# Two halves of a gate weight in one stationary operand, added afterwards by a folding matrix

## The chip, the cores and the metric

The kernel runs on one core of one Trainium2 chip. The metric is the device time of one execution in microseconds (us), the median of three. A core has five engines that run side by side and meet through semaphores: TensorE (PE; its weight loads are listed apart as PEld), VectorE (DVE), ScalarE (ACT), GpSimd (POOL) and SyncE (SP), which here only issues DMAs. Each engine works through its own queue strictly in the order of the program.

## The reference

A decoder trunk of two layers over 256 positions of width 1024. Layer 0 is native sparse attention (NSA): 16 heads in 4 groups, three branches (compressed blocks, selected blocks, sliding window), and three learned gates per head that weight the branches:

```
proj = h @ w_in                      # h = rms_norm(x, norm_w)
q, kc, vc, ks, vs, kw, vw, gl, z = split_cols(proj, ...)
gates = sigmoid(gl)                  # gl: 256 positions x 48 (16 heads x 3)
o = gates0 * o_cmp + gates1 * o_sel + gates2 * o_win
x = x + (o * silu(z)) @ w_out
```

Layer 1 is an HGRN2 gated recurrence with its own input and output projections; a final RMS norm follows. The change touches only `gl` and the sigmoid, 48 columns of the first projection.

## The kernel before, in words

Every large product is made in a split form. A float32 weight tile is copied by ScalarE into a rounded `w_hi` (type fp32r, line 826), VectorE writes the remainder `w_lo = raw - w_hi` (line 1073), and the activations are split in the same way into `h_hi` and `h_lo`. The product is the sum of three passes, hi by hi, hi by lo and lo by hi. The weights come as 19 units of 1024 x 512 through two landing buffers; SyncE may load a unit only when the unit two before it has been split.

One list, `SCHEDULE`, sets the order of all work. It is written out by hand as two strings (`ORDER`, `H_ORDER`), one letter a step, and every engine walks through the same list, doing at each step its own share. Each step fills one of eight PSUM banks; `filled` and `drained` semaphores, one pair a bank, tie TensorE to the engine that empties it. Places for the splits of coming units are given as step numbers, so on ScalarE and VectorE they stand in line with the draining of banks.

The norm's per-position factor `rstd` is not put into `h`: it is a column on positions (`stat[:, 0, 2]`), and a row of it, `rs_row`, serves the outputs that are held transposed.

The steps around the change, in order of the list:

- `wg` (1024 x 48) is loaded (line 509), split by ScalarE (1007) and VectorE (1220).
- `gl` (line 675): for each of 8 slices of the depth, three matmuls with a stationary operand of 48 columns and 256 positions moving: 24 in all, into bank 7, partitions 0 to 47. VectorE multiplies the bank by `rs_row` (1226) and ScalarE writes the sigmoid to `gT` (911).
- `cmpT 0` (659): the compression MLP's hidden layer, whose two halves of 64 partitions are added and transposed in one matmul against `fold`, a 128 x 64 matrix with ones where the partition modulo 64 equals the column. ScalarE takes it with Silu (907).
- `stage 2`: a rotated key tile is transposed (648) and copied out by ScalarE (894).
- `glT` (681): two transposes bring `gT` back to positions x 48; ScalarE copies them to `gate` (914), VectorE masks one branch (1253). The first use of `gate` otherwise is in the attention (1101).
- Then the query units `U_Q0` and `U_Q1`; each of their four tiles passes VectorE (rope, 1194 to 1202), GpSimd (sum, 1427), ScalarE (hi part, 884), GpSimd (lo part, 1435) and is then transposed by TensorE (`stage 4` to `stage 7`). `cmpT 1`, with its Silu, stands between `stage 4` and `stage 5`.
- Line 946 is the exponential of the attention's scores, the first of them at step `s 0`.

Which function set ScalarE has loaded is not written in the kernel: the compiler puts an ACT_TABLE_LOAD ahead of an activation whose function is not in the set that is loaded. Copy never needs one here.

Of the kernel before, what the change touches and what calls it, by code (L numbers as in the profile page):

```python
# [21 lines left out]
P = 128  # L22
D = 1024
S = 256
KT = D // P
TT = S // P
UW = 512
H, G, R, HD = 16, 4, 4, 64
# [9 lines left out]
F32 = mybir.dt.float32  # L38
FR = mybir.dt.float32r
BF16 = mybir.dt.bfloat16  # L40
U8 = mybir.dt.uint8
ALU = mybir.AluOpType
ACT = mybir.ActivationFunctionType
# [3 lines left out]
NSA_Q, NSA_KC, NSA_KS, NSA_KW, NSA_GL, NSA_Z = 0, 1024, 1536, 2048, 2560, 2608  # L47
# [177 lines left out]
def program(nc, t_in, out):  # L225
    with ExitStack() as ctx:
        def sb(name, shape, dt=F32, scope=ctx):
            return scope.enter_context(nc.sbuf_tensor(name, shape, dt))
# [6 lines left out]
        h_hi = sb("h_hi", [P, KT, S], FR)  # L235
        h_lo = sb("h_lo", [P, KT, S], FR)
        g_row = sb("g_row", [P, D])
        g_cols = sb("g_cols", [P, KT])
        ident = sb("ident", [P, P])
        ident_r = sb("ident_r", [P, P], FR)  # L240
        fold = sb("fold", [P, HD])
# [11 lines left out]
        stat = sb("stat", [P, 3, 5, TT])  # L253
# [5 lines left out]
        gate = sb("gate", [P, TT, 48])  # L259
        ostat = sb("ostat", [P, TT, 3, 8])  # L260

        nsa = ExitStack()
# [12 lines left out]
        rs_row, ones = scratch[:, 0:S], scratch[:, S:S + P]  # L275
# [3 lines left out]
        pre = ExitStack()  # L279
# [4 lines left out]
        kcr = sb("kcr", [P, 3, HD], F32, pre)  # L284
        tri = kcr[:, 0:2].rearrange("p a d -> p (a d)")
        kcs = sb("kcs", [P, P], F32, pre)
        wg = sb("wg", [P, KT, 48], F32, pre)
        wg_hi = sb("wg_hi", [P, KT, 48], FR, pre)
        wg_lo = sb("wg_lo", [P, KT, 48], FR, pre)
        gT = sb("gT", [48, S], F32, pre)  # L290
        pre.close()
        att = ExitStack()
        prob_t = sb("prob_t", [P, 4, 512], F32, att)
# [28 lines left out]
        def sem(name):  # L322
            return ctx.enter_context(nc.semaphore(name))
# [13 lines left out]
        wg_in = sem("wg_in")  # L337
# [11 lines left out]
        fold_set = sem("fold_set")  # L349
# [5 lines left out]
        rstd = sem("rstd")  # L355
# [3 lines left out]
        diag_set = sem("diag_set")  # L359
        h0_hi = sem("h0_hi")  # L360
        kc_scaled = sem("kc_scaled")
        gl_scaled = sem("gl_scaled")
        z_scaled = sem("z_scaled")
        r_ab = sem("r_ab")
        r_sum = sem("r_sum")
# [2 lines left out]
        flat_zero = sem("flat_zero")  # L368
        kc_v = sem("kc_v")
        zeros = sem("zeros")  # L370
        wg_hi_d = sem("wg_hi_d")
        wg_lo_d = sem("wg_lo_d")
        gate_v = sem("gate_v")
# [27 lines left out]
        def wait_full(eng, key):  # L401

            b, k = USES[key]
            eng.wait_ge(filled[b], k + 1)

        def wait_taken(eng, key):

            b, k = USES[key]
            eng.wait_ge(drained[b], k + 1)

        def taken(key):
            return drained[USES[key][0]]
# [87 lines left out]
        @block.sync  # L500
        def _(sp):
            for u, (kind, col) in enumerate(UNITS):
                if u == 1:
                    sp.dma_start(rope[:], t_in["c_rope"]).then_inc(rope_in, 16)
                if u == NRAW:
                    for dst, src in CONST_LOADS:
                        sp.dma_start(dst, src).then_inc(const_in, 16)
                if u == NRAW + 1:
                    sp.dma_start(wg[:], t_in["nsa"][:, NSA_GL:NSA_Z].rearrange("(k p) n -> p k n", p=P)).then_inc(wg_in, 16)
                    load_w1(sp, "k")  # L510
                if u >= NRAW:

                    sp.wait_ge(lo_done, split_count(u - NRAW, KT - 1))
                dst = raw[:, u % NRAW]
                w = t_in[kind][:, col:col + UW]
                if kind == "nsa_out":

                    w = w.rearrange("(gp g2 r d) n -> g2 d gp r n", gp=2, g2=2, r=R)
                    for g2 in range(2):
                        for gp in range(2):  # L520
                            sp.dma_start(dst[g2 * HD:(g2 + 1) * HD, gp * R:(gp + 1) * R], w[g2][:, gp]).then_inc(raw_in[u % NRAW], 16)
                    continue
                w = w.rearrange("(k p) n -> p k n", p=P)
                if u == 0:

                    for kk in range(KT):
                        for t, part in {0: ((0, 0),), 1: ((1, 0),), 4: ((0, 1), (1, 1))}.get(kk, ()):
                            half = slice(part * UW, (part + 1) * UW)
                            sp.dma_start(x[:, t, half], t_in["x"][t * P:(t + 1) * P, half]).then_inc(x_in[t][part], 16)
                        sp.dma_start(dst[:, kk], w[:, kk]).then_inc(first_in[kk], 16)  # L530
                    continue
                for half in range(2):
                    landed = second_in[half] if u == 1 else raw_in[u % NRAW]
                    sp.dma_start(dst[:, 4 * half:4 * half + 4], w[:, 4 * half:4 * half + 4]).then_inc(landed, 16)
            for t in range(TT):
                sp.wait_ge(done_row, t + 1)
                sp.dma_start(out[t * P:(t + 1) * P, 0:UW], y_hg[:, t, 0:UW]).then_inc(out_done, 16)
            sp.wait_ge(out_done, 32 * TT)
# [7 lines left out]
        def _(pe):  # L546
            def mm(o, lhsT, rhs, start, stop):
                return nc.tensor.matmul(o, lhsT, rhs, start=start, stop=stop, skip_group_check=True)  # L548
# [16 lines left out]
            for n, (step, banks) in enumerate(SCHEDULE):  # L565
                kind = step[0]
                key = bank_key(step)
# [6 lines left out]
                b, k = USES[key]  # L574
                ps = bank[b]
# [5 lines left out]
                if kind == "hT":  # L581
                    _, L, t, q = step
# [7 lines left out]
                    for j in range(per_bank):  # L590
                        c = (per_bank * q + j) * P
                        m = nc.tensor.transpose(ps[:, j * P:(j + 1) * P], src[:, c:c + P], ident[:])  # L592
                elif kind == "gc":
                    pe.wait_ge(ident_in, 16)
                    pe.wait_ge(g_cols_in, 16)
                    m = nc.tensor.transpose(ps[:, 0:KT], g_rows[0:KT], ident[0:KT, 0:KT])
                elif kind == "rs":
                    pe.wait_ge(ones_set, 1)
                    pe.wait_ge(diag_set, TT)
                    for t in range(TT):  # L600
                        m = mm(ps[:, t * P:(t + 1) * P], ones, diag[:, t], t == 0, t == 1)
                elif kind == "pa" and step[1] == 0:

                    _, u, t, sl = step
# [6 lines left out]
                    for j, kk in enumerate(two):  # L611
# [3 lines left out]
                        m = mm(ps[:], h_lo[:, kk, t * P:(t + 1) * P], w_hi[:, u, kk], False, kk == KT - 1)  # L615
                elif kind == "pa":

                    _, u, t, sl = step
                    if sl == 0:
                        act_ready(0 if u <= U_O1 else 1, t, u)  # L620
                    for kk in (2 * sl, 2 * sl + 1):
# [4 lines left out]
                        m = mm(ps[:], h_lo[:, kk, t * P:(t + 1) * P], w_hi[:, u % 2, kk], False, kk == KT - 1)  # L626
# [48 lines left out]
                elif kind == "gl":  # L675
                    pe.wait_ge(wg_lo_d, 1)
                    for kk in range(KT):
                        mm(ps[0:48, 0:S], wg_hi[:, kk], h_hi[:, kk], kk == 0, False)
                        mm(ps[0:48, 0:S], wg_hi[:, kk], h_lo[:, kk], False, False)
                        m = mm(ps[0:48, 0:S], wg_lo[:, kk], h_hi[:, kk], False, kk == KT - 1)  # L680
                elif kind == "glT":
                    wait_taken(pe, ("gl",))
                    for t in range(TT):
                        m = nc.tensor.transpose(ps[:, t * 48:(t + 1) * 48], gT[:, t * P:(t + 1) * P], ident[0:48, 0:48])
                elif kind == "sc":
                    i = step[1]

# [127 lines left out]
        def _(act):  # L815
# [34 lines left out]
            for n, (step, _) in enumerate(SCHEDULE):  # L850
                kind, key = step[0], bank_key(step)
                if LAST.get(key) == n:
# [54 lines left out]
                        nc.scalar.activation(hidT[:, step[1]].rearrange("p c (g n) -> p (c g) n", g=G)[:, :, 0:CS],  # L907
                                             ps[:, 0:2 * HD].rearrange("p (c n) -> p c n", n=CS), ACT.Silu).then_inc(taken(key), 1)
                    elif kind == "gl":
                        act.wait_ge(gl_scaled, 1)  # L910
                        nc.scalar.activation(gT[:], ps[0:48, 0:S], ACT.Sigmoid).then_inc(taken(key), 1)
                    elif kind == "glT":
                        wait_full(act, key)
                        nc.scalar.activation(gate[:], ps[:, 0:TT * 48].rearrange("p (t c) -> p t c", t=TT), ACT.Copy).then_inc(taken(key), 1)
                    elif kind == "kcT":
                        wait_full(act, key)
                        nc.scalar.activation(kc_t[:], ps[:, 0:P], ACT.Copy).then_inc(taken(key), 1)
# [86 lines left out]
                            nc.scalar.activation(ostat[:, c, 1], ostat[:, c, 0], ACT.Sqrt, scale=1.0 / P, bias=eps_t[:]).then_inc(o_root, 1)  # L1004
                    if key == ("pb", U_KC, 1):
                        act.wait_ge(wg_in, 16)
                        nc.scalar.activation(wg_hi[:], wg[:], ACT.Copy).then_inc(wg_hi_d, 1)
                        act.wait_ge(const_in, 16 * N_CONST)
                        nc.scalar.activation(tri_b[:], tri, ACT.Copy).then_inc(idents, 1)
                    if key == ("pb", V_F0, 0):  # L1010
# [43 lines left out]
        def _(dve):  # L1054
# [11 lines left out]
            V = nc.vector  # L1066
# [82 lines left out]
            for n, (step, _) in enumerate(SCHEDULE):  # L1149
                kind, key = step[0], bank_key(step)  # L1150
                if LAST.get(key) == n:
# [52 lines left out]
                    elif key[0:2] == ("pb", U_KC):  # L1204
# [12 lines left out]
                        m.then_inc(taken(key), 1)  # L1217
                        if kv == 1:
                            dve.wait_ge(wg_hi_d, 1)
                            V.tensor_tensor(wg_lo[:], wg[:], wg_hi[:].bitcast(F32), ALU.subtract).then_inc(wg_lo_d, 1)  # L1220
                            step_(V.tensor_tensor(lb[:, 0], lbl[:, 0], lbl[:, 1], ALU.max))
                            settled()
                            V.tensor_tensor(lb[:, 1:3], lbl[:], bc(lb[:, 0], 2, 1), ALU.subtract).then_inc(lb_v, 1)
                    elif kind == "gl":
                        wait_full(dve, key)
                        V.tensor_tensor(ps[0:48, 0:S], ps[0:48, 0:S], rs_row[0:48], ALU.mult).then_inc(gl_scaled, 1)
                    elif kind == "pb" and step[1] in (U_Z0, U_Z1):
                        wait_full(dve, key)
                        both = lambda ap: ap.rearrange("p (j s) -> p j s", j=2)
# [175 lines left out]
        def _(pool):  # L1405
            GP = nc.gpsimd
            row = lambda ap: ap.unsqueeze(0).broadcast_to([P, D])
            GP.memset(hidT[:], 0.0).then_inc(zeros, 1)
            GP.memset(vc_bd[:], 0.0).then_inc(zeros, 1)

# [110 lines left out]
```

## Time and profile before

| | us |
|---|---|
| three runs | 330.66, 330.60, 330.00; median 330.6 |
| the profiled execution, its own time | 330.72 |
| its span, first to last instruction | 328.9 |
| TensorE busy | 317.3 (96%) |
| VectorE, ScalarE, GpSimd busy | 228.9, 188.6, 57.8 |
| mean granted clock of TensorE | 0.997 of full speed |

Busy time says how full an engine is, not what sets the end. The chain of waits does that: it follows the last instruction back, at each step to what released it. In the rows below the first column is the start of an instruction from the span's start in us, the second its duration in us; `x24` means 24 instructions merged; a bracket at the end gives idle time of the engine before it and what ended that. Line numbers (L548) are those of the kernel before; L548 is the helper that issues every matmul.

### The profile page before, as it was taken

To read this page: it belongs to the slowest core of one execution; us is meant where nothing else is said; L and a number is where in the kernel's file an instruction comes from. 1 tells how busy PE (TensorE), PEld (TensorE's weight loads), DVE (VectorE), ACT (ScalarE), POOL (GpSimd) and SP (SyncE) were. 2 spreads that over 40 slices of the span, in tenths; PEclk is the share of its full clock that TensorE was granted. 3 is DMA by queue.
4 is the path that set the end of the run, shared out by engine and by line. 5 is a ranking of instruction groups with operands and counts; after the bars stand their busy time and mean duration, and the time that the engine had idled before them with its cause. 6 is when DMAs were issued, how large, how long until landed. Compare 5 with 4: busy or idle time off the path is not lost.

```text
span 328.9 us, 6172 instructions
## 1 busy us (share of the span) xinstructions
PE 317.3 (96%) x2380; PEld 268.4 (82%) x2380; DVE 228.9 (70%) x400; ACT 188.6 (57%) x400; POOL 57.8 (18%) x55
## 2 busy tenths in 40 slices
PE   7999999999999999999999999999999999998993
PEld 5889778867989877777678878999999788897882
DVE  2789953649569978879828726277449988489824
ACT  4694355356696666668536706838345036898223
POOL 1004022070423443346300010100000011101000
PEclk9999999999999999999999999999999999999998
DMA  7999999806390920033270773653662424001011
GB/s 229 394 335 209 265 358 195 264 31 223 105 186 0 212 47 2 0 112 146 68 253 0 257 258 127 248 201 91 227 249 91 168 96 165 2 1 66 0 64 64
DMA packets 28828, 49.41 MB, mean 150 GB/s; under 512 B 3256, under 2 KB 7744, under 8 KB 28800
## 3 DMA queue, kind: packets, MB, share of 16 engines
q1 hardware_dynamic: 25760, 44.30, 42.9%
q10 hardware_dynamic: 2528, 2.69, 4.2%
q0 software_dynamic: 512, 2.03, 1.9%
q8 instruction: 19, 0.31, 0.4%
q14 instruction: 9, 0.07, 0.1%
HBM read 47.97 MB, written 1.05 MB: 149 GB/s over the span
## 4 chain that ended last, share of the span: by engine, by line
PE 66%; DVE 16%; ACT 5%; issue 2%; POOL 2%; ACTq 0%; DVEq 0%; POOLq 0%
PE bank L548 61%; DVE w_lo L1073 6%; ACT w_hi L826 3%; PE bank L727 3%; DVE nmax L1268 2%; POOL rp L1427 1%; PE bank L648 1%; DVE prob_t L1280 1%; DVE qk L1357 1%; DVE ft L1324 1%; DVE qk L1343 1%; PE bank L592 1%; DVE zT L1215 1%; DVE zT L1216 0%; ACT prob L946 0%
## 5 line engine op out<-in xcount | busy, mean ns | idle before, releaser
L1073 DVE TENSOR_TENSOR w_lo<-raw,w_hi 128x1024 fp32r<-128x1024 f32 (+1 forms) x80 | 89.2, 1159 | 34.8 <-ACT w_hi L826 34.7
L548 PE MATMUL bank<-w_hi,h_hi 128*128 128x512 f32 x192 | 77.9, 412 | 2.4 <-DVE h_lo L1172 1.1
L548 PE MATMUL bank<-w_hi,h_lo 128*128 128x512 f32 x192 | 75.2, 392 | 0.0
L548 PE MATMUL bank<-w_lo,h_hi 128*128 128x512 f32 x192 | 75.2, 392 | 0.0
L826 ACT ACTIVATE w_hi<-raw 128x1024 fp32r<-128x1024 f32 (+1 forms) x80 | 72.9, 967 | 2.1 <-issue 1.9
L548 PE MATMUL bank<-h_hi,w_hi 128*128 128x256 f32 x224 | 64.9, 290 | 0.1
L548 PE MATMUL bank<-h_hi,w_lo 128*128 128x256 f32 x224 | 63.5, 283 | 0.0
L548 PE MATMUL bank<-h_lo,w_hi 128*128 128x256 f32 x224 | 63.5, 283 | 0.0
L548 PEld LDWEIGHTS bank<-w_hi,h_hi 128*128 128x128 f32 x192 | 35.9, 188 | 11.4 <-issue 4.0
L548 PEld LDWEIGHTS bank<-h_hi,w_hi 128*128 128x128 f32 x224 | 43.0, 192 | 0.5 <-DVE w_lo L1073 0.3
L548 PEld LDWEIGHTS bank<-h_lo,w_hi 128*128 128x128 f32 x224 | 43.0, 192 | 0.3
L548 PEld LDWEIGHTS bank<-h_hi,w_lo 128*128 128x128 f32 x224 | 43.0, 192 | 0.0
L548 PEld LDWEIGHTS bank<-w_hi,h_lo 128*128 128x128 f32 x192 | 36.1, 188 | 7.9
L548 PEld LDWEIGHTS bank<-w_lo,h_hi 128*128 128x128 f32 x192 | 36.2, 188 | 6.8 <-DVE w_lo L1160 0.3
L470 POOL TENSOR_TENSOR prob<-prob,scl 128x512 f32<-128x512 f32 x24 | 28.0, 1166 | 38.9 <-DVE scl L1104 19.8
L946 ACT ACTIVATE prob<-bank,nmax 128x128 f32<-128x128 f32 (+1 forms) x64 | 26.2, 421 | 14.3 <-DVE nmax L1268 14.3
L1427 POOL TENSOR_TENSOR rp<-rp 128x256 f32<-128x256 f32 (+1 forms) x8 | 10.0, 1252 | 64.4 <-DVE rp L1197 44.3
L548 PEld LDWEIGHTS bank<-qk 128*64 128x64 f32 (+1 forms) x496 | 18.0, 140 | 3.8 <-issue 3.5
L548 PE MATMUL bank<-qk 128*64 128x32 f32 (+2 forms) x496 | 19.1, 225 | 0.8 <-DVE qk L1357 0.7
L1456 POOL TENSOR_TENSOR z_hg<-z_hg,g_row 128x512 f32<-128x512 f32 x4 | 5.2, 1301 | 78.9 <-ACT z_hg L967 78.9
L1268 DVE TENSOR_REDUCE nmax<-bank 128x2 f32<-128x512 f32 (+1 forms) x24 | 16.4, 685 | 3.0 <-PE bank L548 2.9
L1357 DVE TENSOR_TENSOR qk<-qk,ft 128x1024 f32<-128x1024 f32 x12 | 15.2, 1284 | 4.1 <-PE bank L548 4.1
(194 smaller groups left out, 424.3 us busy)
## 6 DMA issues: line engine op xcount, KB each, us to landing
raw<-in_hg SPq DMA_DIRECT2D x16, 1024.0 KB, 7.4
raw<-in_nsa SPq DMA_DIRECT2D x12, 1024.0 KB, 9.0
raw<-in_nsa_out SPq DMA_DIRECT2D x8, 512.0 KB, 8.5
raw<-in_hg_out SPq DMA_DIRECT2D x4, 1024.0 KB, 6.2
raw<-in_nsa SPq DMA_DIRECT2D x8, 256.0 KB, 5.9
w<-in_w1k SPq DMA_DIRECT2D x2, 1024.0 KB, 16.3
w<-in_w1v ACTq DMA_DIRECT2D x2, 1024.0 KB, 15.8
x_res<-in_x SPq DMA_DIRECT2D x4, 256.0 KB, 5.2
```

Source lines behind the costliest of these rows:

```text
L470: nc.gpsimd.tensor_tensor(v(pb_), v(pb_), bc(scl[:, it, 0:nb], 512 // nb, 2), ALU.mult).then_inc(scaled, 1)
L548: return nc.tensor.matmul(o, lhsT, rhs, start=start, stop=stop, skip_group_check=True)
L592: m = nc.tensor.transpose(ps[:, j * P:(j + 1) * P], src[:, c:c + P], ident[:])
L648: m = nc.tensor.transpose(ps[:, c * P:(c + 1) * P].bitcast(FR), stg[:, j % 2, 4 * half + c], ident_r[:])
L727: m = nc.tensor.transpose(ps[:, c * P:(c + 1) * P], prob[:, prob_slot(it), c * P:(c + 1) * P], ident[:])
L826: m = nc.scalar.activation(dst, src, ACT.Copy)
L946: m = nc.scalar.activation(prob[:, prob_slot(it), c * w:(c + 1) * w], ps[:, c * w:(c + 1) * w], ACT.Exp, bias=nmax[:, it, c:c + 1], accum_ ...
L1073: m = V.tensor_tensor(lo, src, hi.bitcast(F32), ALU.subtract)
L1268: V.tensor_reduce(nmax[:, it, 0:nb], ps[:].rearrange("p (a b) -> p a b", a=nb), AX.X, ALU.max, negate=True).then_inc(rowmax, 1)
L1357: V.tensor_tensor(both, both, decay, ALU.mult).then_inc(qk_up, 1)
L1427: GP.tensor_tensor(rp[:, 2, 0:w], rp[:, 0, 0:w], rp[:, 1, 0:w], ALU.add).then_inc(r_sum, 1)
L1456: GP.tensor_tensor(zs, zs, g_row[:, (u - V_Z0) * UW:(u - V_Z0 + 1) * UW], ALU.mult).then_inc(z_g, 1)
```

## The change

The high and the low part of the gate weight are put side by side into one tile `wg_r`, 64 columns each (48 of weights, 16 of zeros that GpSimd writes at the start). One matmul with this 128-column operand gives both halves at once, the high part's product on partitions 0 to 47, the low part's on 64 to 111; it is made with `h_hi` and with `h_lo`. ScalarE copies the bank out unscaled. In `glT` a matmul against the first 48 columns of `fold` adds the halves and transposes. `rstd` is now a per-partition scale of the sigmoid, which therefore comes behind `glT`, once for each 128 positions.

```diff
-        wg = sb("wg", [P, KT, 48], F32, pre)
-        wg_hi = sb("wg_hi", [P, KT, 48], FR, pre)
-        wg_lo = sb("wg_lo", [P, KT, 48], FR, pre)
-        gT = sb("gT", [48, S], F32, pre)
+        wg = sb("wg", [P, KT, HD], F32, pre)
+        wg_r = sb("wg_r", [P, KT, 2, HD], FR, pre)
+        gT = sb("gT", [P, S], F32, pre)
...
                 elif kind == "gl":
                     pe.wait_ge(wg_lo_d, 1)
                     for kk in range(KT):
-                        mm(ps[0:48, 0:S], wg_hi[:, kk], h_hi[:, kk], kk == 0, False)
-                        mm(ps[0:48, 0:S], wg_hi[:, kk], h_lo[:, kk], False, False)
-                        m = mm(ps[0:48, 0:S], wg_lo[:, kk], h_hi[:, kk], False, kk == KT - 1)
+                        both = wg_r[:, kk].rearrange("p a c -> p (a c)")
+                        mm(ps[:, 0:S], both, h_hi[:, kk], kk == 0, False)
+                        m = mm(ps[:, 0:S], both, h_lo[:, kk], False, kk == KT - 1)
                 elif kind == "glT":
                     wait_taken(pe, ("gl",))
+                    pe.wait_ge(fold_set, 1)
                     for t in range(TT):
-                        m = nc.tensor.transpose(ps[:, t * 48:(t + 1) * 48], gT[:, t * P:(t + 1) * P], ident[0:48, 0:48])
+                        m = mm(ps[:, t * 48:(t + 1) * 48], gT[:, t * P:(t + 1) * P], fold[:, 0:48], t == 0, t == TT - 1)
...
                     elif kind == "gl":
-                        act.wait_ge(gl_scaled, 1)
-                        nc.scalar.activation(gT[:], ps[0:48, 0:S], ACT.Sigmoid).then_inc(taken(key), 1)
+                        wait_full(act, key)
+                        nc.scalar.activation(gT[:], ps[:, 0:S], ACT.Copy).then_inc(taken(key), 1)
                     elif kind == "glT":
                         wait_full(act, key)
-                        nc.scalar.activation(gate[:], ps[:, 0:TT * 48].rearrange("p (t c) -> p t c", t=TT), ACT.Copy).then_inc(taken(key), 1)
+                        act.wait_ge(rstd, TT)
+                        nc.scalar.activation(gate[:, 0], ps[:, 0:48], ACT.Sigmoid, scale=stat[:, 0, 2, 0:1])
+                        nc.scalar.activation(gate[:, 1], ps[:, 48:96], ACT.Sigmoid, scale=stat[:, 0, 2, 1:2]).then_inc(taken(key), 1)
...
                         act.wait_ge(wg_in, 16)
-                        nc.scalar.activation(wg_hi[:], wg[:], ACT.Copy).then_inc(wg_hi_d, 1)
+                        act.wait_ge(wg_pad, 1)
+                        nc.scalar.activation(wg_r[:, :, 0], wg[:], ACT.Copy).then_inc(wg_hi_d, 1)
...
-                            V.tensor_tensor(wg_lo[:], wg[:], wg_hi[:].bitcast(F32), ALU.subtract).then_inc(wg_lo_d, 1)
+                            V.tensor_tensor(wg_r[:, :, 1], wg[:], wg_r[:, :, 0].bitcast(F32), ALU.subtract).then_inc(wg_lo_d, 1)
...
-                    elif kind == "gl":
-                        wait_full(dve, key)
-                        V.tensor_tensor(ps[0:48, 0:S], ps[0:48, 0:S], rs_row[0:48], ALU.mult).then_inc(gl_scaled, 1)
...
+            GP.memset(wg[:, :, 48:HD], 0.0).then_inc(wg_pad, 1)
             GP.memset(hidT[:], 0.0).then_inc(zeros, 1)
```

The load of `wg` writes 48 of each 64 columns; otherwise it is as before.

## Rows read from the trace of the kernel before

**Rows 1.** Page, part 4: shares of the chain that ended last, by engine

```profile
PE 66%; DVE 16%; ACT 5%; issue 2%; POOL 2%; ACTq 0%; DVEq 0%; POOLq 0%
```

**Rows 2.** Chain of waits, 40 to 92 us: start, duration, engine and line

```profile
40.63 15.28 PE bank L548 x96
...
56.20 0.25 PE bank L684 x2
...
74.36 0.28 ACT hid L900
...
75.87 5.98 PE bank L548 x28
...
85.75 0.30 PE bank L648 x4
```

**Rows 3.** Timeline of TensorE around 22, 50 and 56 us (start, duration, ...)

```profile
21.57 0.28 PE L548 MATMUL bank<-h_lo,w_hi 128*128 128x256 f32 x1
...
22.27 0.28 PE L548 MATMUL bank<-h_lo,w_hi 128*128 128x256 f32 x1
...
48.38 0.12 PEld L548 LDWEIGHTS bank<-h_lo,wg_hi 128*48 128x48 f32 x1
...
50.95 0.12 PEld L548 LDWEIGHTS bank<-h_hi,wg_lo 128*48 128x48 f32 x1
...
51.18 0.55 PE L548 MATMUL bank<-fold,hid 128*128 128x64 f32 x4
...
51.54 0.48 PE L548 MATMUL bank<-w_hi,h_hi 128*128 128x512 f32 x1
...
56.13 0.32 PE L684 MATMUL bank<-ident,gT 48*128 48x48 f32 x2
...
56.38 0.54 PE L648 MATMUL bank<-ident_r,stg 128*128 128x128 f32 x4
```

**Rows 4.** Timeline of ScalarE, 51 to 62 us

```profile
51.84 0.38 ACT L911 ACTIVATE gT<-bank 48x256 f32<-48x256 f32 x1 [2.05 <-DVE bank L1226]
...
52.23 1.28 ACT L907 ACT_TABLE_LOAD   x1
...
53.53 0.28 ACT L907 ACTIVATE hidT<-bank 128x128 f32<-128x128 f32 x1
...
58.09 0.24 ACT L914 ACTIVATE gate<-bank 128x96 f32<-128x96 f32 x1
...
61.88 0.60 ACT L894 ACTIVATE k<-bank 128x512 fp32r<-128x512 f32 x1 [3.05 <-PE bank L648]
```

**Rows 5.** One source line, L962 (F: sigmoid, Q: silu, in turn)

```profile
L962 ACT ACT_TABLE_LOAD  x4: 1283/1283/1283, 207.2 to 242.3; - x4
```

**Rows 6.** Timeline of ScalarE, 77 to 84 us

```profile
77.25 0.60 ACT L894 ACTIVATE q<-bank 128x512 fp32r<-128x512 f32 x1
77.72 0.29 ACT L907 ACTIVATE hidT<-bank 128x128 f32<-128x128 f32 x1
77.88 1.17 ACT L826 ACTIVATE w_hi<-raw 128x512 fp32r<-128x512 f32 x2
...
83.27 0.63 ACT L884 ACTIVATE stg<-rp 128x512 fp32r<-128x512 f32 x1 [3.73 <-POOL rp L1427]
```

**Rows 7.** Timeline of VectorE, 63 to 80 us

```profile
63.39 0.75 DVE L1194 SCALAR_TENSOR_TENSOR rp<-bank,stat,rope 128x512 f32<-128x512 f32 x1 [3.04 <-PE bank L548]
...
79.08 1.29 DVE L1073 TENSOR_TENSOR w_lo<-raw,w_hi 128x512 fp32r<-128x512 f32 x2 [0.23 <-ACT w_hi L826]
80.29 0.75 DVE L1194 SCALAR_TENSOR_TENSOR rp<-bank,stat,rope 128x512 f32<-128x512 f32 x1
```

**Rows 8.** Timeline of GpSimd, 81 to 86 us

```profile
81.90 1.28 POOL L1427 TENSOR_TENSOR rp<-rp 128x512 f32<-128x512 f32 x1 [8.07 <-DVE rp L1202]
83.98 1.30 POOL L1435 TENSOR_TENSOR stg<-rp,stg 128x512 fp32r<-128x512 f32 x1 [0.80 <-ACT stg L884]
```

**Rows 9.** Timeline of TensorE's weight loads, 85 us

```profile
85.40 0.51 PEld L648 LDWEIGHTS bank<-ident_r,stg 128*128 128x128 f32 x4
```

More of the change, by code:

```diff
@@ L361, in program @@
         kc_scaled = sem("kc_scaled")
-        gl_scaled = sem("gl_scaled")
         z_scaled = sem("z_scaled")
@@ L370, in program @@
         zeros = sem("zeros")
+        wg_pad = sem("wg_pad")
         wg_hi_d = sem("wg_hi_d")
@@ L508, in _ @@
                 if u == NRAW + 1:
-                    sp.dma_start(wg[:], t_in["nsa"][:, NSA_GL:NSA_Z].rearrange("(k p) n -> p k n", p=P)).then_inc(wg_in, 16)
+                    sp.dma_start(wg[:, :, 0:48], t_in["nsa"][:, NSA_GL:NSA_Z].rearrange("(k p) n -> p k n", p=P)).then_inc(wg_in, 16)
                     load_w1(sp, "k")
```

## The prediction, made before the changed kernel was run

> **What bounds the kernel now.** I read the page's chain by engine first: TensorE holds 66% of it, VectorE 16%, ScalarE 5% [rows 1]. So a matmul saved is worth something only where TensorE's work is the piece that ends last, and a ScalarE instruction costs something only where it delays such a piece. Next the chain in order of time. From 40.63 us TensorE is on it without a break for 15.28 us, which takes in the gate's 24 matmuls, and the two gate transposes at 56.20 are on it as well. Then a stretch runs through VectorE, GpSimd and ScalarE and comes back through `hid` at 74.36; from 75.87 TensorE has it again, the transposes of `stage 6` at 85.75 among them [rows 2]. The reader is to see that everything the change touches lies within this half, and that the chain starts each link from TensorE: VectorE's rope at 63.39 waited 3.04 us for a TensorE bank [rows 7]. No DMA holds a share of the chain [rows 1].
>
> **What is removed on TensorE.** The 24 gate passes follow one another every 0.117 us: the second weight load starts at 48.38, the last at 50.95, 22 steps, 2.57 us [rows 3]. Would a full operand of 128 columns be slower? Passes of just that form (128 columns held, 256 moving) near 22 us stand at 21.57 and 22.27 with six steps between: 0.117 us as well [rows 3]. So the width costs nothing, the 16 passes take 1.87 us where 24 took 2.81, and 0.94 us goes. If the wider load cost something, the gain would be less; bound from below nothing, from above 0.94. I take 0.94, since the row is of the same form.
>
> **What is added in `glT`.** Two transposes become two float32 matmuls against `fold`. The same form with 64 moving columns stands at `cmpT 0`: it starts at 51.18 and the next work at 51.54, 0.36 us for two calls (four instructions). The old pair took from 56.13 to 56.38, 0.25 us [rows 3]. That is +0.11; with 48 columns a little less. I take +0.1 (bounds 0 and +0.2). TensorE is then 0.84 us early from 56.4 on.
>
> **Edits with cost nothing.** VectorE loses the product with `rs_row`, and ScalarE no longer waits for it; both stood idle there (ScalarE 2.05 us before `gT` [rows 4]), so nothing is gained. The two wider splits of `wg` add a third to one instruction each, long before `gl`, and the pad memset is GpSimd's first instruction, on an engine with nothing to do then. The new waits (`fold_set`, `wg_pad`, `rstd`) are for things done tens of microseconds earlier. The `wg` load moves the same bytes. If TensorE's later work should come to wait for a split, the wider split costs at most about 0.15 us.
>
> **The function sets of ScalarE.** Before, the order is sigmoid (`gl`), silu (`cmpT 0`), silu (`cmpT 1`), exp. Between sigmoid and silu there is a load of 1.28 us at 52.23, and between the two silus none: at 77.72 the second follows the copy at 77.25 directly [rows 4, 6]. After the change the order is silu (`cmpT 0`), sigmoid (`glT`), silu (`cmpT 1`), exp. Could one set hold both functions? Layer 1 changes from sigmoid to silu, back, and over again, and line 962 has four loads for it [rows 5]; so no set that the compiler picks holds both, in either direction. The number of loads thus goes up by one, and two stand in new places.
>
> The first, ahead of the sigmoid, meets idle time. `gate` was written at 58.09 and after the next copy ScalarE waited 3.05 us for TensorE, until 61.88 [rows 4]. A load (1.28) and one more activation (about 0.3) fit into 3.05; without that cover they would cost 1.6. Queued behind them are one key copy, whose reader comes much later, and VectorE's mask and its small key work, followed by a wait of 3.04 us [rows 7]. The copy of `gT` needs no load, so the silu behind it comes earlier than before. Nothing is lost here.
>
> The second, ahead of the silu of `cmpT 1`, does not. ScalarE is busy without a gap there. Before, the silu starts 0.47 us after the copy at 77.25, overlapping it. A load does not overlap: at 51.84 `gT` ran 0.38 us, the load began at 52.23, and the next activation at 53.53, 1.30 us later [rows 4]. So the silu will start 0.60 + 1.30 = 1.90 us after the copy starts, 1.43 us later than it did [rows 6]. Behind it in ScalarE's queue stands the split at 77.88, and what follows has no slack at all: VectorE waited 0.23 us for that split and starts the remainder at 79.08; its rope at 80.29 stands directly behind [rows 7]; GpSimd waited 8.07 us for the rope and starts at 81.90 [rows 8]; ScalarE waited 3.73 us for GpSimd and starts the hi part at 83.27 [rows 6]; GpSimd makes the lo part from 83.98 to 85.28 [rows 8]; and TensorE loads the operand of `stage 6` at 85.40 [rows 9], 0.12 us after. Other such releases take about 0.07, so TensorE had 0.05 us to spare.
>
> **The sum.** ScalarE comes to 77.25 earlier by 0.84 (the whole chain up to there starts from TensorE) and leaves the silu later by 1.43: net +0.59 at the split, and this +0.59 is handed along to 85.28. Less the 0.05 of slack, `stage 6` starts 0.54 us later than before, though TensorE is ready for it 0.84 us earlier: it will stand idle some 1.4 us between 82 and 86. `stage 6` is on the chain [rows 2], so +0.54 goes to the end: 330.72 + 0.54 = 331.26 on the profiled execution, which is 0.12 above the median of the runs; on the median, 331.1 us. The own range of this case is +0.2 to +0.9: the gain at TensorE may be 0.74 to 0.94, and the load's 1.28 may overlap its neighbours by some tenths.
>
> **A rule weighed.** What the rows show is a load of 1.28 us with the next activation 0.02 us behind its end [rows 4]. The Trainium skill, ScalarE: Activation LUTs, section "What ACT_TABLE_LOAD costs", gives the same 1283 ns but adds a drain of about 1380 ns, some 2.66 us for each switch, and its section on table sets says to batch calls by set, which this change undoes. By that price the sum would be an estimate of +1.9 us, 332.5. The trace has no such drain at this place, so I give it little.
>
> **The rivals.**
> - A. The second load does not reach TensorE: a set with both functions is found, or the split behind the silu has more room than I see. Then only TensorE's gain is left, 330.6 - 0.84 = 329.8. For it: TensorE's 0.84 is sure. Against it: four loads at line 962 [rows 5] and a queue without gaps [rows 6 to 8].
> - B, the slower side. The load is paid and the gain is not had: between 56 and 74 us something that does not start from TensorE sets the pace, so that ScalarE reaches the copy at 77.25 when it did before. The price is the load's 1.43 less 0.05, +1.38, 332.0. It decides as soon as such a link is up to 0.84 us late against TensorE. For it: this stretch of the chain goes over three engines and a landed weight. Against it: VectorE's 3.04 us wait for TensorE at its head [rows 7].
> - C. The two cancel: the load overlaps, or later stretches where VectorE and ScalarE set the pace take up half: -0.3 to +0.2, about 330.6.
> - D. After a load ScalarE has to wait as long again as the load: 0.54 + 1.28 = +1.82, 332.4. Against it the 0.02 us in the row [rows 4]. (This is the drain of the skill's page ScalarE: Activation LUTs.)
>
> **How the numbers follow.** Forecast 0.60, A 0.13, B 0.12, C 0.11, D 0.04. About 0.2% (0.66 us) is what a measurement of this kernel can tell from no change. The forecast's +0.54 lies near this bound: of its 0.60 I put 0.38 within and 0.22 above. Faster is A with a little more, 0.14. Slower is 0.22 + B + D = 0.38. Within is 0.38 + C, 0.48 after rounding. The range reaches from A with its gain in full (-0.9, 329.7) to B (332.0) with a tenth on top: 329.7 to 332.1; the likeliest case's own is 330.8 to 331.5.
>
> **What would show each step.** Sixteen gate passes 0.117 us apart and the work behind `gl` 0.9 us earlier. ScalarE's loads at `cmpT 0`, at `glT` and at `cmpT 1`, one more in all than before. No wait of TensorE for `stage 2` or `stage 3`. `hid` of `cmpT 1` about 0.84 us before 74.36; the split that was at 77.88 at about 78.5; TensorE idle for over a microsecond shortly before `stage 6`, released by VectorE or GpSimd, and `stage 6` at about 85.95; from there all starts about half a microsecond later. If `cmpT 1` has no load, rival A holds and the forecast is wrong in sign; if `hid` is not early, B holds; if the load is there and `stage 6` is not later than 85.4, I have misread the slack of the rope chain.

## The result, and the profile after

The changed kernel takes 331.97 us (median of 7 runs, 331.47 to 333.51) against 330.52 before (7 runs, 330.00 to 330.66). The ratio of the runs is 1.0050, 95% interval 1.0035 to 1.0066: slower by 0.5%, or by 1.45 us (0.44%) between the medians. The forecast was 331.1, an added 0.54 us, just under the 0.66 us that it took as the least a measurement can tell from no change. The profiled execution took 332.11 us, its span is 330.3 (before 330.72 and 328.9).

Page, part 4, of the changed kernel, as in [rows 1]: TensorE has lost four points of the chain.

```profile
PE 62%; DVE 16%; ACT 7%; issue 3%; POOL 3%; ACTq 0%; DVEq 0%; POOLq 0%
```

Its chain of waits in order of time (start, duration, engine and line), which answers to [rows 2]. Line numbers of the changed kernel differ a little: L547 is the helper of every matmul, L647 the transposes of the stages. Two pieces are new: a function-set load of ScalarE (ACT L907 at 76.92) with the split, rope, sum and lo part behind it, down to `stage 6` at 85.88; and at 275.30 a piece called "issue", 1.08 us in which TensorE waited for nothing that the profile shows.

```profile
40.48 14.38 PE bank L547 x88
...
73.41 0.27 ACT hid L900
...
76.92 1.28 ACT L907
78.21 0.28 ACT hidT L907
...
82.38 1.28 POOL rp L1428
...
84.45 1.29 POOL stg L1436
...
85.88 0.51 PE bank L647 x4
...
270.89 4.41 PE bank L547 x91
275.30 1.08 issue
276.38 10.69 PE bank L547 x131
```

TensorE's weight loads around `gl` and `glT`, as in [rows 3] (start, duration, engine, line): 16 loads, the first at 48.00 and the last at 49.89, then `cmpT 0`; the loads of `gT` at 54.96, the next stage's at 55.34.

```profile
48.00 0.19 PEld L547 LDWEIGHTS bank<-h_hi,wg_r 128*128 128x128 f32 x1
48.24 0.19 PEld L547 LDWEIGHTS bank<-h_lo,wg_r 128*128 128x128 f32 x1
...
49.89 0.19 PEld L547 LDWEIGHTS bank<-h_lo,wg_r 128*128 128x128 f32 x1
50.01 0.53 PEld L547 LDWEIGHTS bank<-fold,hid 128*128 128x128 f32 x4
...
54.96 0.52 PEld L547 LDWEIGHTS bank<-fold,gT 128*128 128x128 f32 x4
55.34 0.47 PEld L647 LDWEIGHTS bank<-ident_r,stg 128*128 128x128 f32 x4
```

ScalarE's timeline, as in [rows 4]: the load ahead of the gates' sigmoid lies in what was idle time, of which 1.49 us is left at 60.92.

```profile
56.56 0.58 ACT L894 ACTIVATE k<-bank 128x512 fp32r<-128x512 f32 x1
57.16 1.28 ACT L915 ACT_TABLE_LOAD   x1
58.45 0.30 ACT L915 ACTIVATE gate<-bank,stat 128x48 f32<-128x48 f32 x1
...
60.92 0.60 ACT L894 ACTIVATE k<-bank 128x512 fp32r<-128x512 f32 x1 [1.49 <-PE bank L647]
```

ScalarE, as in [rows 6]: the second load, 76.92, between the copy and the silu.

```profile
76.30 0.60 ACT L894 ACTIVATE q<-bank 128x512 fp32r<-128x512 f32 x1
76.92 1.28 ACT L907 ACT_TABLE_LOAD   x1
78.21 0.28 ACT L907 ACTIVATE hidT<-bank 128x128 f32<-128x128 f32 x1
78.39 1.14 ACT L826 ACTIVATE w_hi<-raw 128x512 fp32r<-128x512 f32 x2
...
83.75 0.63 ACT L884 ACTIVATE stg<-rp 128x512 fp32r<-128x512 f32 x1 [3.73 <-POOL rp L1428]
```

VectorE, as in [rows 7]: the wait for the split has grown from 0.23 to 1.65 us.

```profile
79.56 1.29 DVE L1076 TENSOR_TENSOR w_lo<-raw,w_hi 128x512 fp32r<-128x512 f32 x2 [1.65 <-ACT w_hi L826]
80.77 0.74 DVE L1197 SCALAR_TENSOR_TENSOR rp<-bank,stat,rope 128x512 f32<-128x512 f32 x1
```

TensorE's weight load of `stage 6`, as in [rows 9], at 85.85 where it was at 85.40.

```profile
85.85 0.40 PEld L647 LDWEIGHTS bank<-ident_r,stg 128*128 128x128 f32 x4 [0.57 <-issue]
```

The start of a run differs from one profiled execution to the next: the first gate weight load, to which no edit below matters, came between 47.48 and 48.67 us. So places are compared from that load on. Each number is a start in the kernel's own trace less the start of its first gate weight load: the `hid` activation of `cmpT 1`, the first weight load of `stage 6`, the last sigmoid of layer 1 (`F`). The column "end" is the end of the last instruction on the same scale, and the ratio is that of the runs against the kernel before in its own group of runs.

| kernel | `hid`, `cmpT 1` | `stage 6` | layer 1, last `F` | end | ratio (95%) |
|---|---|---|---|---|---|
| before | 26.12 | 37.25 | 193.51 | 280.77 | |
| changed | 25.32 | 37.85 | 193.75 | 282.30 | 1.0050 (1.0035 to 1.0066) |
| `e1_pad6` | 25.32 | 37.86 | 193.77 | 281.04 | 1.0017 (1.0004 to 1.0030) |
| `e3_load_late` | 25.31 | 37.85 | 193.73 | 281.08 | 1.0014 (1.0005 to 1.0022) |
| `e4_before_minus6` | 25.42 | 36.57 | 192.76 | 281.36 | 1.0013 (1.0001 to 1.0026) |
| `e7_before_loads` | 26.12 | 38.66 | 194.78 | 282.02 | 1.0030 (1.0018 to 1.0043) |
| `e2_one_set_pad6` | 25.32 | 36.87 | 193.02 | 280.27 | 0.9988 (0.9980 to 0.9997) |
| `f1_one_set_pad6` | 25.31 | 36.46 | 192.54 | 279.77 | 0.9977 (0.9969 to 0.9986) |
| `f2_sigmoid_only_pad6` | 25.31 | 36.46 | 192.40 | 279.70 | 0.9980 (0.9971 to 0.9989) |
| `f3_sigmoid_only_late` | 25.32 | 36.47 | 192.45 | 279.67 | 0.9973 (0.9964 to 0.9982) |
| `f6_before_late` | 26.12 | 37.27 | 193.40 | 280.71 | 1.0001 (0.9992 to 1.0010) |

The changed kernel against the kernel before reads: 0.80 early at `hid`, 0.60 late at `stage 6`, only 0.24 late in layer 1, and 1.53 late at the end. So the first half of the story is as forecast, something is given back between, and 1.29 us come in after 242 us, in a stretch that the change does not touch. Each row is one trace; against what the ratios give, the ends in the table are off by up to 0.4 us, so they say where time comes in and not how much to a tenth.

The hole: TensorE's weight loads in the level products of layer 1, kernel before, then changed kernel. 64 tiny loads of one step, which run in one piece before, are cut after 53.

```profile
273.49 1.95 PEld L548 LDWEIGHTS bank<-qk 128*64 128x64 f32 x64 [0.37 <-issue]
```

```profile
273.54 1.65 PEld L547 LDWEIGHTS bank<-qk 128*64 128x64 f32 x53 [0.36 <-issue]
276.38 0.43 PEld L547 LDWEIGHTS bank<-qk 128*64 128x64 f32 x11 [1.19 <-issue]
```

What else differs there is in the DMA view. Each queue is a line: packets, MB, share of the engines. Queue q8 carries 19 packets of instructions, 0.31 MB, over the whole run in both kernels. TensorE has 2380 matmuls and as many weight loads, 4760 instructions; 4760 over 19 packets is 250 each, so q8 reads as TensorE's program coming in blocks of about 250 (a reading: the trace does not name the engine that a packet is for). In the kernel before, one of them starts at 267.0 us, on an idle DMA system; its window is 266 to 267 us:

```profile
q8 instruction: 1, 0.02, 5.7%
```

In the changed kernel this packet starts at 273.8 us, within the last weight load, the 2 MB of `V_O1` (queue q1), and 1.5 us before the hole; window 273 to 274 us:

```profile
q1 hardware_dynamic: 188, 0.39, 102.9%
q8 instruction: 1, 0.02, 6.8%
```

The change leaves TensorE with 2374 matmuls: eight gate passes less, two more instructions in `glT`. With the weight loads its program is 12 instructions shorter from `glT` on, and the blocks end 12 instructions later in the kernel's work.

The packet and the load stand in the same relation to the hole in all 14 traces of this case. In the changed kernel, in `e4_before_minus6` and in `e6b_order` the packet starts 5.0 to 5.1 us after the load's first packet; these three have the hole, and their load takes 7.6 to 7.7 us from its first packet to its last. In the other 11 the packet has landed before the load's first packet starts; none has the hole, and the load takes 6.1 to 6.3 us.

### The profile page after: what moved, and what is told of

It is laid out like the page before. It is cut to its first block, busy times and chain, and to the rows that moved or that the text cites. A ratio compares the mean times of both kernels' runs of the same rounds, so it can differ in the third digit from the quotient of the medians.

```text
span 330.3 us, 6164 instructions
## 1 busy us (share of the span) xinstructions
PE 316.9 (96%) x2374; PEld 267.5 (81%) x2374; DVE 228.3 (69%) x399; ACT 190.5 (58%) x402; POOL 57.0 (17%) x56
## 4 chain that ended last, share of the span: by engine, by line
PE 62%; DVE 16%; ACT 7%; issue 3%; POOL 3%; ACTq 0%; DVEq 0%; POOLq 0%
PE bank L547 57%; DVE w_lo L1076 6%; ACT w_hi L826 4%; PE bank L727 2%; POOL rp L1428 2%; DVE nmax L1268 1%; PE bank L647 1%; POOL stg L1436 1%; DVE qk L1357 1%; ACT prob L948 1%; DVE ft L1324 1%; DVE qk L1343 1%; DVE prob_t L1280 1%; PE bank L591 1%; DVE zT L1218 1%
## 5 line engine op out<-in xcount | busy, mean ns | idle before, releaser
L547 PE MATMUL bank<-w_hi,h_hi 128*128 128x512 f32 x192 | 77.8, 411 | 2.3 <-DVE h_lo L1175 1.1
L547 PE MATMUL bank<-w_hi,h_lo 128*128 128x512 f32 x192 | 75.2, 392 | 0.0
L547 PE MATMUL bank<-w_lo,h_hi 128*128 128x512 f32 x192 | 75.0, 391 | 0.0
L547 PE MATMUL bank<-h_hi,w_hi 128*128 128x256 f32 x224 | 64.8, 289 | 0.6 <-DVE vc_bd L1246 0.6
L547 PE MATMUL bank<-h_hi,w_lo 128*128 128x256 f32 x224 | 63.4, 283 | 0.0
L547 PE MATMUL bank<-h_lo,w_hi 128*128 128x256 f32 x224 | 63.3, 283 | 0.0
L547 PEld LDWEIGHTS bank<-w_hi,h_hi 128*128 128x128 f32 x192 | 35.9, 188 | 11.3 <-issue 4.0
L547 PEld LDWEIGHTS bank<-h_hi,w_hi 128*128 128x128 f32 x224 | 42.9, 192 | 1.5 <-DVE vc_bd L1246 1.0
L547 PEld LDWEIGHTS bank<-h_lo,w_hi 128*128 128x128 f32 x224 | 42.9, 192 | 0.2
L547 PEld LDWEIGHTS bank<-h_hi,w_lo 128*128 128x128 f32 x224 | 42.9, 192 | 0.0
L547 PEld LDWEIGHTS bank<-w_hi,h_lo 128*128 128x128 f32 x192 | 36.0, 188 | 7.9
L547 PEld LDWEIGHTS bank<-w_lo,h_hi 128*128 128x128 f32 x192 | 36.1, 188 | 6.9 <-DVE w_lo L1163 0.4
L469 POOL TENSOR_TENSOR prob<-prob,scl 128x512 f32<-128x512 f32 x24 | 27.1, 1127 | 39.6 <-DVE scl L1107 20.5
L547 PEld LDWEIGHTS bank<-qk 128*64 128x64 f32 (+1 forms) x496 | 18.1, 139 | 5.0 <-issue 4.7
L547 PE MATMUL bank<-qk 128*64 128x32 f32 (+2 forms) x496 | 19.3, 225 | 1.9 <-issue 1.1
```

Source lines behind the costliest of these rows:

```text
L469: nc.gpsimd.tensor_tensor(v(pb_), v(pb_), bc(scl[:, it, 0:nb], 512 // nb, 2), ALU.mult).then_inc(scaled, 1)
```

## The experiments

**Is it the fetch?** Theory F (fetch) and rival L (load) are named in the first expectation below. `e1_pad6` gives TensorE the missing instructions back and nothing else; they stand at `cmpT 1`, where it waits for `hid` anyway.

```diff
                 elif kind == "cmpT":
                     kv = step[1]
+                    if kv == 1:
+                        for _ in range(6):
+                            mm(ps[:, 0:16], ident_r[:], ident_r[:, 0:16], True, True)
```

> The changed kernel with six tiny matmuls (16 columns) put in where TensorE waits for `hid` of `cmpT 1`, so that TensorE's program is again as long as before from there on (the change took out six matmuls and six weight loads). Theory F (fetch): the 1.08 us hole at 275.3 us comes from a block of TensorE's instructions fetched behind the 2 MB load of `in_hg_out`, because the shorter program asks for it about 12 instructions later. Then the hole goes, the fetch is back at about 267 us, and the time is 331.97 - 1.1 = 330.9. Rival L (load): the whole +1.45 comes from the function-set load in front of `cmpT 1` and what it triggers; the hole stays or another takes its place, 332.0.

Measured 331.20 us against 330.64. The trace shows no hole; the step runs in one piece again, here in TensorE's weight loads:

```profile
274.27 1.95 PEld L547 LDWEIGHTS bank<-qk 128*64 128x64 f32 x64 [0.36 <-issue]
```

All places up to layer 1 are those of the changed kernel within 0.02 us, and the end comes 1.26 us earlier. The packet of q8 is back ahead of the load: it starts at 268.1, the load's first packet at 269.5. Theory F holds, rival L falls. By the ratios the hole is worth 1.0050 - 1.0017 = 0.33%, 1.1 us; the medians against their own groups give 0.9 us (1.45 less 0.56). The time is 0.3 us above the 330.9 that F expected.

`e3_load_late` leaves the program short and takes away what the fetch would meet.

```diff
+                if u == V_O1:
+                    sp.wait_ge(qk_up, 6)
                 dst = raw[:, u % NRAW]
```

> The changed kernel, only the last weight load (`V_O1`, 2 MB) held back about 2 us, until the sixth product of the levels, so that it starts at about 270.8 us in place of 268.1. Its first use is at about 287 us. Theory F: the instruction fetch asked for at about 268.3 us no longer stands behind the load, the hole at 275.3 goes, 330.9. Rival L: nothing changes, 332.0. A third: a later load collides with the next fetch instead, and a hole of about 1 us turns up elsewhere, 332.

Measured 331.10 us, no hole. The load's first packet starts at 272.0, where it was 268.8 in the changed kernel, so it was held back by 3.3 us and not 2. The packet of q8 now comes on an idle DMA system within 270 to 271 us, at 270.5; that of the changed kernel came at 273.8, so it was some 3.4 us late. (I had put its due time at about 268.3; it is some 2 us later.)

```profile
q8 instruction: 1, 0.02, 7.5%
```

`f6_before_late` is the control, the same late load in the kernel before.

> Control: the kernel before with the last weight load held back in the same way. It has no hole, so theory F expects 330.6, no change. If the late load were worth something by itself (then `e3` would not speak for the fetch), 329.7 or less.

Measured 330.39 against 330.62, ratio 1.0001 (0.9992 to 1.0010): the late load by itself is worth nothing that can be measured. So what it gave the changed kernel was the hole.

`e4_before_minus6` goes the other way and makes the hole in the kernel before.

```diff
-                        mm(ps[0:48, 0:S], wg_hi[:, kk], h_lo[:, kk], False, False)
+                        if kk >= 6:
+                            mm(ps[0:48, 0:S], wg_hi[:, kk], h_lo[:, kk], False, False)
```

> The kernel before with six of the 24 gate passes left out (the high-by-low pass of the first six slices; the gates are less exact). No function-set load moves. Theory F: TensorE is 0.7 us early behind `gl`, but its program is shorter by the same 12 instructions, so the hole of 1.0 to 1.2 us at about 275 turns up here too: 330.5 - 0.5 + 1.1 = 331.1. Rival L: only the gain, 329.8 to 330.3, no hole.

Measured 331.09 us against 330.64, ratio 1.0013. Six gate passes fewer make the kernel slower, by 0.45 us. TensorE's weight loads show the cut at the same place, after 53 of the 64:

```profile
272.46 1.65 PEld L548 LDWEIGHTS bank<-qk 128*64 128x64 f32 x53 [0.36 <-issue]
275.31 0.43 PEld L548 LDWEIGHTS bank<-qk 128*64 128x64 f32 x11 [1.21 <-issue]
```

In layer 1 it is 0.75 us ahead of the kernel before, at the end 0.59 behind: the hole and what follows cost 1.34.

**What do the function-set loads cost?** `e7_before_loads` puts both of them into the kernel before, by a second sigmoid on top of the first; it is a probe of time, its gates are not those of the reference.

```diff
-   nc.scalar.activation(gate[:], ps[:, 0:TT * 48].rearrange(...), ACT.Copy)
+   nc.scalar.activation(gate[:], ps[:, 0:TT * 48].rearrange(...), ACT.Sigmoid)
```

> The kernel before, the copy of `gate` made a sigmoid (a second one on top of the first, so the gates are wrong in value). This brings both new function-set loads, at `glT` and at `cmpT 1`, and no change on TensorE, whose program keeps its length. By the prediction's steps: `stage 6` starts 1.38 us late and no hole at 275. If that delay goes to the end whole: 331.9; theory F, by which some 0.2 us of a delay at 118 to 124 us is absorbed: 331.6. If the loads cost nothing (all of the +1.45 is the hole): 330.5.

Measured 331.75 against 330.64, ratio 1.0030. `stage 6` is 1.41 us late (expected 1.38), the end 1.25 us late by the trace and 1.11 by the medians, no hole. That lies between the 331.9 of a delay handed on whole and the 331.6 with part of it absorbed, and decides nothing between them.

`e2_one_set_pad6` and `f1_one_set_pad6` are the other half: TensorE's saving without the load. Silu stands where the gates need sigmoid, so these too are probes of time. Shown is the first of the two lines; the second is changed in the same way.

```diff
-   nc.scalar.activation(gate[:, 0], ps[:, 0:48], ACT.Sigmoid, scale=stat[:, 0, 2, 0:1])
+   nc.scalar.activation(gate[:, 0], ps[:, 0:48], ACT.Silu, scale=stat[:, 0, 2, 0:1])
```

> The changed kernel with silu in place of the two sigmoids of the gates (wrong gates), so that no other function set is needed between `cmpT 0` and `cmpT 1`, and with the six tiny matmuls that keep TensorE's program as long as before. It is TensorE's saving alone. By the prediction's steps, counted from the first gate weight load: `stage 6` 0.8 us earlier than before (36.4 against 37.25), with no load at `cmpT 1`. If that passes to the end, 330.64 - 0.8 = 329.8. If later stretches set by VectorE and ScalarE give no room to a gain, 330.4.

Measured 330.24 us, `stage 6` at 36.87 and not 36.4. My own padding was in the way: placed behind TensorE's wait for bank 6, the six matmuls could start only when `hid` had been taken, and pushed `cmpT 1` back. In `e1` the same delay had been hidden under the wait for ScalarE.

> As `e2_one_set_pad6` (silu for the gates' sigmoids, wrong gates, no load between the two silus), but the six tiny matmuls now stand ahead of TensorE's wait for bank 6, so that they fill time in which it waits for `hid`. In `e2` they ran behind it and cost about 0.45 us on the path: its `stage 6` came at 36.87 us from the first gate load and not at 36.4. Expected now 36.4, and 330.24 - 0.45 = 329.8. If the 0.45 went elsewhere, 330.2 again.

Measured 329.87 us against 330.62, `stage 6` at 36.46, with the matmuls ahead of that wait. TensorE's saving alone brings 0.79 us at `stage 6` and 0.75 us (0.23%) at the median.

**A version that has the gain.** The first try moved `cmpT 0` behind `glT`, so that the functions come as sigmoid, silu, silu. In the order string (cut at both ends):

```diff
-...FFFGkFIIgJgkKK...
+...FFFGFIIgJkgKKk...
```

> The changed kernel with its sigmoids kept, and `cmpT 0` moved from behind `gl` to behind `glT` (`cmp2 0` two steps later). The functions then come as sigmoid, silu, silu, exp: three loads as before, none in front of `cmpT 1`. TensorE's program padded to its old length. If the load in front of `cmpT 1` is what cost 1.43 us on ScalarE: `stage 6` at about 36.4 from the first gate load, 329.8, faster than before. If the moved silu makes TensorE wait at `cmp2 0`, or the key copies come late: 330.3.

> The same order without the padding. Theory F: the loads' cost is gone but TensorE's program is 12 instructions short, so the hole at about 275 is there: 329.8 + 1.3 = 331.1. If the hole depended on how late the whole is against the last weight load, and not on the length of the program, there is none: 329.8.

> The same order without the padding, and the last weight load held back until the sixth product of the levels. Theory F: no hole, 329.8, as with the padding. Else 331.1.

A miss: 334.54, 335.36 and 333.47 us, ratios 1.0122, 1.0146 and 1.0090. ScalarE's timeline of `e6_order_pad6` shows two loads nearly end to end, so that `hidT` is ready only at 60.15:

```profile
56.77 1.28 ACT L918 ACT_TABLE_LOAD   x1
...
58.27 0.29 ACT L919 ACTIVATE gate<-bank,stat 128x48 f32<-128x48 f32 x1
58.58 1.28 ACT L910 ACT_TABLE_LOAD   x1
59.87 0.28 ACT L910 ACTIVATE hidT<-bank 128x128 f32<-128x128 f32 x1
```

and TensorE, in order, waits for it at `cmp2 0` (its weight loads, with the wait in brackets):

```profile
60.26 0.52 PEld L547 LDWEIGHTS bank<-w,hidT 128*128 128x128 f32 x4 [1.89 <-ACT hidT L910]
```

`hid` of `cmpT 1` comes 27.83 us after the first gate load, 2.51 later than in the changed kernel, and the end of `e6_order_pad6` (284.18 on the table's scale) 3.14 later than that of `e1_pad6`. In this group too the trace of the short program without the late load (`e6b`) has the hole, 1.08 us after 53 of the 64 loads, and the other two have none; but its span (331.5) was no longer than theirs (332.2 and 331.4), the runs of `e6b` spread from 332.93 to 336.76, and what else differs between the three I did not follow up.

The second try keeps the order and avoids silu before the attention. It is the changed kernel with

```diff
-   ps[:, 0:2 * HD]..., ACT.Silu).then_inc(taken(key), 1)
+   ps[:, 0:2 * HD]..., ACT.Sigmoid).then_inc(hid_sig, 1)
...
+            def hid_times(kv):
+                key = ("cmpT", kv)
+                dve.wait_ge(hid_sig, kv + 1)
+                v = hidT[:, kv].rearrange("p c (g n) -> p (c g) n", g=G)[:, :, 0:CS]
+                V.tensor_tensor(v, v, bk(key)[:, 0:2 * HD].rearrange("p (c n) -> p c n", n=CS), ALU.mult).then_inc(taken(key), 1)
```

> The changed kernel with right gates and one function set: the two silus of the compression become a sigmoid on ScalarE and a product with the bank on VectorE (about 0.25 us each; the second just before the remainder split that was at 79.08). Loads: sigmoid, exp. TensorE's program padded to its old length, in the idle time before `cmpT 1`. If the second load is what turned the gain of 0.84 us into a loss: `stage 6` at 36.4 to 36.7 from the first gate load, 329.8 to 330.1, faster than before. If the product on VectorE delays the rope chain by its whole 0.25 us plus a handover: 330.3.

Measured 329.78 against 330.62, ratio 0.9980. No hole. ScalarE and VectorE of this kernel: no load between the copy and the activation, and the product fits into VectorE's old 0.23 us wait for the split.

```profile
76.39 0.60 ACT L899 ACTIVATE q<-bank 128x512 fp32r<-128x512 f32 x1
76.87 0.29 ACT L912 ACTIVATE hidT<-bank 128x128 f32<-128x128 f32 x1
77.03 1.17 ACT L831 ACTIVATE w_hi<-raw 128x512 fp32r<-128x512 f32 x2
```

```profile
77.92 0.28 DVE L1161 TENSOR_TENSOR hidT<-hidT,bank 128x128 f32<-128x128 f32 x1
78.24 1.29 DVE L1081 TENSOR_TENSOR w_lo<-raw,w_hi 128x512 fp32r<-128x512 f32 x2
```

> The same without padding, with the last weight load held back until the sixth product of the levels in its place. Theory F: no hole at about 275, the same time as with padding, 329.8 to 330.1; with the hole 331.2.

Measured 329.69 us, ratio 0.9973, no hole. Both are faster than the kernel before (by 0.2 and 0.27%) and than the changed one by 0.7%; the two ways past the hole can't be told apart.

## Why the prediction was wrong

Point by point, with the prediction's own steps:

- **The gate passes**: right. From the second load (48.24) to the last (49.89) are 14 steps, 0.118 us each, where 0.117 was taken. From the first gate load to that of `cmpT 0` it is 2.01 us, 0.91 less than before.
- **`glT`**: right in size, +0.1. At `hid` 0.80 us of the 0.84 are there.
- **One more load, two in new places, the first under idle time**: right. Line 907 has two loads and line 915 one. VectorE's mask waited 0.64 us for it and nothing later shows it.
- **The load in front of `cmpT 1` delays the silu by 1.43**: right. It starts 1.91 us after the copy starts (78.21 less 76.30) where 0.47 was. `e7` has it alone: 1.41 us at `stage 6`.
- **`stage 6` 0.54 us late**: 0.60. TensorE stood idle in two places, not in one: it also waited 1.0 us for VectorE to empty bank 6 (line 1246), which stands behind the rope in VectorE's queue.
- **The rule weighed**: the drain that the Trainium skill, ScalarE: Activation LUTs, section "What ACT_TABLE_LOAD costs" adds to each load is not there: load at 57.16, next activation at 58.45; load at 76.92, next at 78.21. Rival D is out. Its other rule, to batch calls by set, is borne out by `e7` and `f2`.
- **"So +0.54 goes to the end"**: this step failed, on both sides. The delay reached layer 1 as 0.24 us, and then 1.29 us were added. The sum at the end is 0.24 + 1.29 = 1.53 where 0.54 stood (1.45 between the medians).

Of the 0.36 us given back, 0.12 are gone at the next transposes after `stage 6` (41.98 before and 42.46 in the changed kernel, from the first gate load) and 0.22 go at 118 to 124 us. In the kernel before, GpSimd's scaling at 120.99 and VectorE's split at 120.89 started together and both were slow. GpSimd, then VectorE, of the kernel before:

```profile
120.99 2.02 POOL L470 TENSOR_TENSOR prob<-prob,scl 128x512 f32<-128x512 f32 x1 [0.80 <-DVE scl L1104]
```

```profile
120.89 3.21 DVE L1073 TENSOR_TENSOR w_lo<-raw,w_hi 128x1024 fp32r<-128x1024 f32 x2
```

In the changed kernel VectorE waits 0.35 us for ScalarE's later split, GpSimd has begun by then, and both are quicker, 1.04 and 2.99 us. GpSimd, then VectorE:

```profile
120.95 1.04 POOL L469 TENSOR_TENSOR prob<-prob,scl 128x512 f32<-128x512 f32 x1 [0.43 <-DVE scl L1107]
```

```profile
121.22 2.99 DVE L1076 TENSOR_TENSOR w_lo<-raw,w_hi 128x1024 fp32r<-128x1024 f32 x2 [0.35 <-ACT w_hi L826]
```

That is read from the two traces and was not tested by itself.

The part added is the hole. It is not a wait of the kernel's and so stood in no step and no rival. The prediction had read that no DMA holds a share of the chain; that holds for both kernels, since the hole stands in the chain as "issue", and so the chain did not show how near a packet of instructions lay to a load. It counted each removed instruction by its time and not by its place in the program: "eight passes fewer" also moved all later block limits of TensorE's instruction stream by 12 instructions, and one packet with them from 267.0 us, ahead of the last 2 MB load, to about 270.5 (`e3`), after that load's first packet at 268.8. `e1`, `e3`, `e4` and the control `f6` show this from four sides. Why 12 instructions moved the packet by 3.5 us, more than the 1.4 us of six matmuls at the 0.23 us each that they took there, stays open: when exactly TensorE asks for a block is not in the records; that the packet waits behind the load's packets is read from its late arrival in the changed kernel and in `e4` and its early one in `e3`.

Rival B had the price nearest to the result (332.0), by another mechanism: its mark, a late `hid`, did not come, and the nearness is chance. Rival C's mechanism, a later stretch that takes up part of the delay, did act. Without the hole the forecast would have looked right: `e1` and `e3` measure 0.56 and 0.46 us above the kernel before between the medians, where 0.54 stood. Their traces end only 0.27 and 0.31 us late, so how much of the 0.54 arrives is not settled, and that agreement is no proof of the step.

## What to carry to other kernels

Before moving a nonlinear function past others on the same engine, list the functions in program order and count the set changes; one load between two tight pieces cost more (1.43 us) than the eight matmuls saved (0.91). A program that is otherwise equal can gain or lose about a microsecond when its length changes ahead of a stretch of many tiny instructions that runs beside a large transfer; look for a piece called "issue" in the chain and for the instruction queue's packets beside it, and pad the program or move the transfer before judging the edit.

## What the runs showed of the hardware

- Packets of instructions (q8; TensorE's, by their number) share the DMA engines with the weights: with one of them inside, a load of 2 MB took 7.6 to 7.7 us, without 6.1 to 6.3. On idle engines the packet came nearly 5 us before the place where it is missed in the changed kernel (270.5 in `e3` against 275.3) and nothing stalled; when it came at 273.8 us and landed at 274.9, TensorE ran dry at 275.30 and went on at 276.38. The hole was 1.08, 1.10 and 1.08 us in three kernels (changed, `e4`, `e6b`), always after 53 of 64 loads, and 1.3 us with what followed in the first two. Why TensorE goes on only 1.4 to 1.5 us after the packet has landed, about when the load's last packet moves (276.4), is open.
- A function-set load took 1.28 us each time, and the next activation, where it waited for nothing else, followed 0.01 to 0.02 us behind its end; what it takes away beside its length is the overlap of neighbouring activations (0.15 us here: 1.43 in all).
- The width of the stationary operand cost nothing in a stream of passes of 256 moving columns: with 128 columns, whose loads take 0.19 us, they stand 0.118 us apart, with 48 columns and loads of 0.12 us 0.117.
